# A two-block transformer on one core: gate decays made beside the projection, a gate bias spread in one matmul, row steps placed in VectorE's waits

## The reference, cut to what matters

```python
h = x @ w_in[l]                                  # all columns of the three mixers
# spatial gate: 4 heads of 64, chunks of 128 tokens
v = layer_norm(v, ln_g, ln_b);  w = where(tril, w_s, 0)
z = einsum('hij,bnjhd->bnihd', w, v) + b_s.T[:, :, None];  out_a = u * z
# gated delta rule: 8 heads of 64, chunks of 64
q, k, v = split(silu(causal_short_conv(qkv, conv_w)));  q, k = l2_norm(q) * 64**-0.5, l2_norm(k)
sol = triangular_solve(eye + lower, rhs);  ... then a recurrence over the chunks
# gated attention: 4 heads, keys of 32, values of 64, chunks of 64
log_a = log_sigmoid(g_low @ gate_up + gate_b) / 16
bcum = cumsum(log_a, within a chunk)
q_dec, k_inv, k_dec = q*exp(bcum), k*exp(-bcum), k*exp(bcum[-1]-bcum)
```

## Time and profile before

| | us |
|---|---|
| median of three executions | 3999.43 (3999.33 to 4000.17) |
| profiled execution, its own time | 3998.43 |
| span of the profiled execution, first to last instruction | 3996.6 |
| PE busy | 3807.0 (95%) |
| DVE busy | 2082.7 (52%) |
| ACT busy | 1382.5 (35%) |
| mean granted clock of TensorE, as a share of 2.4 GHz | 0.951 |

### The profile page before, as it was taken

The page is one execution under the profiler, slowest core; times in us unless marked ns, Lnnn a source line. Parts: engine busy times, 40 slices in busy tenths (PEclk is TensorE's granted clock), DMA queues, the critical chain, the costliest instruction groups (busy, mean ns, idle before and its releaser), DMA issues.

```text
span 3996.6 us, 44618 instructions
## 1 busy us (share of the span) xinstructions
PE 3807.0 (95%) x18516; PEld 3137.8 (79%) x18516; DVE 2082.7 (52%) x3673; ACT 1382.5 (35%) x2100; POOL 86.4 (2%) x164
## 2 busy tenths in 40 slices
PE   8998989999999999999999988999999999899998
PEld 5975489999986688888887766888788877577886
DVE  5936757644456543333347467433633374756335
ACT  5434533212356432322226424222322255233222
POOL 0100001111000000000000000000000000000000
PEclk9998999999999999999999958999999999679999
DMA  6410014433320122232222201222222222002222
GB/s 225 151 43 1 1 43 132 125 127 127 103 69 22 43 95 95 99 109 100 96 95 81 78 1 43 95 95 97 85 100 95 96 84 81 15 33 85 95 99 81
DMA packets 92877, 333.35 MB, mean 83 GB/s; under 512 B 11362, under 2 KB 11522, under 8 KB 92420
## 3 DMA queue, kind: packets, MB, share of 16 engines
q1 hardware_dynamic: 77040, 278.10, 20.2%
q0 software_dynamic: 12800, 41.95, 3.4%
q10 hardware_dynamic: 2836, 10.44, 0.7%
HBM read 328.35 MB, written 2.10 MB: 83 GB/s over the span
## 4 chain that ended last, share of the span: by engine, by line
PE 89%; DVE 5%; ACT 5%; issue 1%; DMA 0%; DVEq 0%; ACTq 0%; SPq 0%
PE PS L511 73%; PE PS L1078 2%; PE PS L513 2%; PE PS L1063 1%; PE PS L1094 1%; PE PS L1066 1%; PE PS L1424 1%; PE PS L944 0%; PE PS L2372 0%; PE PS L2168 0%; PE PS L1395 0%; PE PS L716 0%; PE PS L1995 0%; ACT XH L891 0%; DVE H_r L680 0%
## 5 line engine op out<-in xcount | busy, mean ns | idle before, releaser
L511 PE MATMUL PS<-arena_r,ring_hi 128*128 128x512 f32 (+1 forms) x6224 | 2106.0, 377 | 71.2 <-DVE H_r L680 70.1
L511 PE MATMUL PS<-arena_r,ring_r 128*128 128x512 f32 (+1 forms) x4752 | 1781.4, 375 | 0.0
L511 PEld LDWEIGHTS PS<-arena_r,ring_hi 128*128 128x128 f32 x6224 | 1168.4, 189 | 253.3 <-DVE H_r L680 61.9
L511 PE MATMUL PS<-H_r,ring_hi 128*128 128x512 f32 (+1 forms) x3280 | 1231.3, 375 | 0.0
L511 PEld LDWEIGHTS PS<-arena_r,ring_r 128*128 128x128 f32 x4752 | 897.6, 189 | 131.9
L380 DVE TENSOR_TENSOR ring_r<-ring,ring_hi 128x1024 fp32r<-128x1024 f32 x514 | 627.7, 1222 | 660.5 <-ACT ring_hi L371 660.0
L371 ACT ACTIVATE ring_hi<-ring 128x1024 fp32r<-128x1024 f32 x514 | 541.9, 1056 | 875.3 <-DMA ring<-weights_dram 867.5
L511 PEld LDWEIGHTS PS<-H_r,ring_hi 128*128 128x128 f32 x3280 | 622.9, 190 | 95.5 <-issue 3.1
L1654 ACT ACTIVATE arena<-PS 128x512 f32<-128x512 f32 x88 | 52.7, 598 | 532.6 <-PE PS L511 532.6
L1232 DVE SCALAR_TENSOR_TENSOR XH<-PS,mods,XH 128x256 f32<-128x256 f32 (+1 forms) x144 | 68.5, 524 | 237.3 <-PE PS L511 237.3
L1658 DVE SCALAR_TENSOR_TENSOR arena<-arena,PS 128x512 f32<-128x512 f32 x88 | 60.5, 688 | 225.8 <-PE PS L511 225.8
(11 more groups left out here) (370 smaller groups left out, 3164.2 us busy)
## 6 DMA issues: line engine op xcount, KB each, us to landing
ring<-weights_dram SPq DMA_DIRECT2D x526, 512.0 KB, 3.2
rstd<-ada_later_dram POOLq DMA_DIRECT2D x54, 256.0 KB, 2.9
mean<-ada_later_dram POOLq DMA_DIRECT2D x53, 256.0 KB, 3.0
ada_extra<-ada_later_dram POOLq DMA_DIRECT2D x53, 256.0 KB, 3.0
XH<-xT_dram ACTq DMA_DIRECT2D x1, 3072.0 KB, 20.2
ring<-weights_dram ACTq DMA_DIRECT2D x4, 512.0 KB, 4.1
out_dram<-XH SPq DMA_DIRECT2D x8, 256.0 KB, 2.0
con<-second_dram ACTq DMA_DIRECT2D x1, 1536.0 KB
```

The source lines that it names most:

```text
L511: ins = pe.matmul(PS[:, o.bank, 0:hi - lo], w[:, 0, :], x, **flags)
```

## The change

What it does, in the order of the diff:

1. In the projection the gate matmul of the gated attention is issued beside tile 4, the gate logs (four activations) beside tile 5 on ACT, and the minimum, the scaling and the running sum beside tile 6 on DVE. Results go to `silu_ctx` and `ada_extra`. They leave the shared stage.
2. The row turn, the key turn and the value turn, with what ACT and DVE do for them, are written one tile later.
3. The bias of the spatial gate is loaded as two rows, and one matmul for each half of the heads writes it into the bank before the products, which add to it; the products of the two heads of a half alternate.
4. On DVE the weights are masked before the wait for ACT's compaction, and the row steps are divided differently among the other parts: 2, 5, 5, 6 and 13 in place of 10, 14 and 7.

```diff
@@ in_plan
+            t[4]["beside_pe"] = lambda pe: gla_gate_pe(pe, l, gates)
+            t[5]["beside_act"] = lambda act: gla_gate_act(act, l)
+            t[6]["beside_dve"] = lambda dve: gla_gate_dve(dve)
...
-            t[14]["beside_pe"] = lambda pe: turn_rows_pe(pe, l)
-            t[15]["beside_act"] = lambda act: (turned_rows_act(act), high_rows_act(act))
-            t[16]["beside_pe"] = lambda pe: turn_keys_pe(pe, l)
-            t[17]["beside_dve"] = lambda dve: (key_rows_dve(dve, l), low_rows_dve(dve))
-            t[19]["beside_pe"] = lambda pe: turn_values_pe(pe, l)
-            t[20]["beside_dve"] = value_rows_dve
+            t[15]["beside_pe"] = lambda pe: turn_rows_pe(pe, l)
+            t[16]["beside_act"] = lambda act: (turned_rows_act(act), high_rows_act(act))
+            t[17]["beside_pe"] = lambda pe: turn_keys_pe(pe, l)
+            t[18]["beside_dve"] = lambda dve: (key_rows_dve(dve, l), low_rows_dve(dve))
+            t[20]["beside_pe"] = lambda pe: turn_values_pe(pe, l)
+            t[21]["beside_dve"] = value_rows_dve
...
+        gate_arg, gate_log = silu_ctx[:, 0:512], silu_ctx[:, 512:1024]
+        def gla_gate_pe(pe, l, gates):
+            pe.wait_ge(small_loaded.sem, 64 + 48 * l)
+            pe.wait_ge(evac["dve"].sem, gates.freed)
+            pe.matmul(PS[:, 0, :], gup[0:16, :], gl[0:16, :], start=True, stop=True).then_inc(ga_low.sem, 1)
+        def gla_gate_act(act, l):
+            act.wait_ge(ga_low.sem, ga_low.next("act"))
+            a_link(act, nc.scalar.activation(gate_arg, PS[:, 0, :], ACT.Identity, bias=V("gla_gb", l)))
+            a_link(act, nc.scalar.activation(gate_log, gate_arg, ACT.Abs))
+            a_link(act, nc.scalar.activation(gate_log, gate_log, ACT.Exp, scale=-1.0))
+            nc.scalar.activation(gate_log, gate_log, ACT.Ln, bias=V("one")).then_inc(ga_log.sem, 1)
+        def gla_gate_dve(dve):
+            dve.wait_ge(ga_log.sem, ga_log.next("dve"))
+            v_link(dve, nc.vector.scalar_tensor_tensor(out=gate_arg, in0=gate_arg, scalar=0.0, in1=gate_log, op0=ALU.min, op1=ALU.subtract))
+            v_link(dve, nc.vector.tensor_scalar(gate_log, gate_arg, 1.0 / 16.0, None, ALU.mult))
+            nc.vector.tensor_tensor_scan(ada_extra[:], C("rs64", 0, 512), gate_log, 0.0, ALU.mult, ALU.add)
...
+        PAIR = con2_r[:, SELP:SELP + P].bitcast(F32)
...
-        bc, e1, e2, kdec = (area(4096 + 512 * i, 512) for i in range(4))
+        bc = ada_extra[:]
+        _, e1, e2, kdec = (area(4096 + 512 * i, 512) for i in range(4))
@@ units_pe
-            pe.wait_ge(small_loaded.sem, 64 + 48 * l)
-            pe.matmul(PS[:, 4, :], gup[0:16, :], gl[0:16, :], start=True, stop=True).then_inc(ga_low.sem, 1)
...
-            for h in range(4):
-                o = 64 * (h % 2)
+            for q in range(2):
+                pe.matmul(PS[:, q, :].rearrange("p (n t) -> p n t", n=NLT), PAIR[0:2], bs_row[0:2, P * q:P * q + P].unsqueeze(1).to_broadcast([2, NLT, P]),
+                          start=True, stop=False, skip_group_check=True)
                 for n in range(NLT):
-                    dst = PS[o:o + 64, h // 2, P * n:P * n + P]
-                    pe.matmul(dst, vt(n, slice(64 * h, 64 * h + 64)), wsT[:, h, :], start=True, stop=False)
-                    ins = pe.matmul(dst, C("ones")[0:1, 0:64], bs_row[0:1, P * h:P * h + P], start=False, stop=True)
+                    for j in range(2):
+                        h = 2 * q + j
+                        ins = pe.matmul(PS[64 * j:64 * j + 64, q, P * n:P * n + P], vt(n, slice(64 * h, 64 * h + 64)), wsT[:, h, :],
+                                        start=False, stop=True, skip_group_check=True)
@@ units_act
-            act.wait_ge(so_ld.sem, so_ld.next("act"))
-            act.wait_ge(ga_low.sem, ga_low.next("act"))
-            a_link(act, nc.scalar.activation(bc, PS[:, 4, :], ACT.Identity, bias=V("gla_gb", l)))
-            a_link(act, nc.scalar.activation(e1, bc, ACT.Abs))
-            a_link(act, nc.scalar.activation(e1, e1, ACT.Exp, scale=-1.0))
-            nc.scalar.activation(e1, e1, ACT.Ln, bias=V("one")).then_inc(ga_log.sem, 1)
@@ gla_decay_dve
-            dve.wait_ge(ga_log.sem, ga_log.next("dve"))
-            v_link(dve, nc.vector.scalar_tensor_tensor(out=bc, in0=bc, scalar=0.0, in1=e1, op0=ALU.min, op1=ALU.subtract))
-            v_link(dve, nc.vector.tensor_scalar(e2, bc, 1.0 / 16.0, None, ALU.mult))
-            v_link(dve, nc.vector.tensor_tensor_scan(bc, C("rs64", 0, 512), e2, 0.0, ALU.mult, ALU.add))
@@ solve_dve
+            mask_w_dve(dve, l)
             dve.wait_ge(so_d.sem, so_d.next("dve", 4))
-            nc.vector.transpose(LD, D_.rearrange("p q (j t) -> p t q j", j=8)).then_inc(so_ld.sem, 1)
+            ins = nc.vector.transpose(LD, D_.rearrange("p q (j t) -> p t q j", j=8))
+            ins.then_inc(so_ld.sem, 1)
+            dve.wait_ge(so_ld.sem, so_ld.next("dve"))
             centre_v_dve(dve)
+            rows_dve_of_inverse(dve, 0, 2)
             gla_decay_dve(dve)
-            mask_w_dve(dve, l)
+            rows_dve_of_inverse(dve, 2, 7)
             norm_v_dve(dve, l)
             gla_products_dve(dve)
-            rows_dve_of_inverse(dve, 0, 10)
+            rows_dve_of_inverse(dve, 7, 12)
             gla_states_dve(dve)
-            rows_dve_of_inverse(dve, 10, 24)
+            rows_dve_of_inverse(dve, 12, 18)
             sgu_out_dve(dve)
             gla_mask_dve(dve)
-            rows_dve_of_inverse(dve, 24, 31)
+            rows_dve_of_inverse(dve, 18, 31)
@@ third_loads
-                act.dma_start(bs_row[0:1, :], sgub_d[l:l + 1]).then_inc(small_loaded.sem, 16)
+                act.dma_start(bs_row[0:2, 0:2 * P], sgub_d[l].rearrange("(q j t) -> j q t", q=2, j=2)).then_inc(small_loaded.sem, 16)
```

## The result

| | before | after |
|---|---|---|
| median on one chip, us | 3999.38 (3996.74 to 4000.17, 4 executions) | 3972.28 (3964.97 to 3974.40, 4 executions) |
| ratio after to before, 95% interval | | 0.9931 (0.992 to 0.9943) |
| profiled execution, its own time / span, us | 3998.43 / 3996.6 | 3964.97 / 3963.2 |
| DVE busy, ACT busy, us | 2082.7, 1382.5 | 2080.1, 1388.4 |
| mean granted clock of TensorE | 0.951 | 0.957 |

27.1 us less; forecast were 31.4 less, 3968.0. The number came out close, but not by the steps that were forecast. The table cuts both profiles at the same points of the program; a cell gives the length before, then after.

The account below looks back on a forecast made before the run. PE was taken to bound the shared stage in one layer, DVE in the other, with PE waiting for ACT's roots in the projection. 2 x 5.09 + 1.7 + 8.1 + 2.07 + 9.4 = 31.4 us less, 3968.0; range 3960 to 3979.

Parts of the forecast that it names:

- Row turn a tile later: Projection: PE's 4.48 us wait for ACT's roots and 1.65 us of slow clock behind it go, 6.13 us a layer.
- the rival in which ACT comes late to it: Projection: ACT's roots come late to the row turn, 4.0 to 7.3 us lost in both layers, 3972 to 3975; chance 0.10.
- Gate work in the projection: Gate matmul beside tile 4 costs 1.04 us a layer; 6.4 us of gate logs fit 7.3 us of ACT's cover.
- Start of the shared stage: Up to the scaling of v: 1.7 us less in the first layer, 2.07 us in the second.
- Mixing: Spatial gate on PE, shared stage: 9.2 us in place of 17.3; bounds 5 at the higher clock, 12.8 to 14.
- Halves overlap; that rival: Mixing: the rival said halves don't overlap, 12.8 to 14 us in place of 9.2, total 3975 to 3978; chance 0.10.
- Row steps: DVE, shared stage: steps moved into its waits; second layer's scaling of v to output takes 22.9 us, 9.4 less.
- the rival in which the steps only change places: Shared stage: edits do nothing because another engine waits next; only the projection's 10.2 us remain, 3989; chance 0.04.
- Behind the output: End of the shared stage: length kept, as the inverses are there 1.3 us before the 12.57 us of output end.
- the quicker: Output and behind: TensorE's faster clock is granted sooner, 1.3 and 3 us better a layer, 3959 to 3965; chance 0.12.
- slower rival: Behind the output: clock stays at 1.2 GHz, 16.8 us more a layer plus mix projection tiles, up to 4034; chance 0.03.
- The sum: Both layers together: 31.4 us less, 3967.0 by the profiled execution, 3968.0 by the median; given 0.61.

Follow-up runs that it names:

- run 3: Changed kernel with ScalarE making the high half of tile 16's weight slab ahead of the second roots, not behind them: 3964.30 us, ratio 0.992.
- run 4: Changed kernel with both sets of gate logs made together beside tile 5 and none beside tile 8: 3963.65 us, ratio 0.9918.
- run 9: Changed kernel with the gated attention's gate matmul, logs and running sum back at the start of the shared stage: 3975.03 us, ratio 0.9946.
- run 10: The kernel of run 3 with two more of VectorE's row steps (12 and 13) ahead of the states: 3963.21 us, ratio 0.9906.
- run 5: Changed kernel with the mixing loop and bias load of before, each product followed by its own bias matmul: 3987.04 us.
- run 6: Changed kernel with VectorE's row steps divided as before (0 to 10, 10 to 24, 24 to 31): 3992.73 us.
- run 2: Kernel before with only the row, key and value turns moved a tile later: 3995.09 us, ratio 0.9991.

## Why the prediction came out as it did

**Row turn a tile later (-6.1 a layer): the step that failed.** The text had the wait go with 0.97 us to spare, and of what follows it said that the inputs keep their distance and that the weight halves "are made three slabs ahead of PE". For the row turn the reckoning was right: PE begins it at 2212.02 with no idle time ahead, so the rival in which ACT comes late to it did not occur. But the text asked which instructions read the roots, and not what stands behind the roots in ACT's list. By the trace of before the new wait could have been had. There the chain has the roots (start us, us, what):

```profile
2213.12 2.20 ACT arena L1738 x4
```

and the timeline of DVE the low half of tile 16's slab, which ends at 2219.9:

```profile
2218.71 1.23 DVE L380 TENSOR_TENSOR ring_r<-ring,ring_hi 128x1024 fp32r<-128x1024 f32 x1 [9.38 <-ACT ring_hi L371]
```

PE ends tile 14 at 2215.36 - 4.48 = 2210.9, so it would ask for tile 16 at 2210.9 + 5.45 + 0.66 = 2217.0; the slab follows the roots (end 2215.3) by a load, an evacuation, a silu, a high and a low half, 1.28 + 0.60 + 0.52 + 0.95 + 1.24 = 4.6, thus 2219.9. That is a wait of 2.9 us; 3.2 were measured, with the slow clock behind it. Runs 3 and 4 give 4.9 and 4.8 us a layer back, each by another edit.

**Gate work in the projection.** Right. The matmul takes 1.05 us (forecast 1.04), and ACT's second roots end 1.2 us later, of which 1.05 are PE's. ACT's idle time covered the logs. Each load again takes 1.28 us with the next activation 0.01 us behind it, so the drain of 1.38 us that the Trainium skill (ScalarE: Activation LUTs, "What ACT_TABLE_LOAD costs") adds to a load shows in no row here either.

**Start of the shared stage.** Right: 1.5 and 2.1 us against 1.7 and 2.07, and run 9 loses 2.2. Steps 0 to 7 fit ahead of the scaling of v, with 3.0 us of DVE's wait left there. The "over 7 us" that DVE was said to wait was a misreading: it idled 1.31 and 3.46 us in the first layer, and 7 is reached only with the 2.4 us of the three instructions that leave.

**Mixing: the term that was mis-sized.** 9.2 us were taken, at 1.2 GHz throughout; it took 4.2, at a granted clock of 1.00, which is under even the 5 that the text gave as its bound for the quick clock. At 1.2 GHz (run 10) it takes 7.9: the bias matmuls 2.07 each as forecast, four alternating pairs 1.98, thus 0.49 a pair in place of the 0.63 to 0.70 read from L1991. So PE isn't the later engine in the first layer, and the stretch is DVE's 22.8 in place of 25.1, 2.2 us better than the sum. Halves overlap; that rival is out: in the kernel before, where products did not alternate, a single one already took 0.62 us from its start to the next start at that clock:

```profile
2350.99 0.69 PE L1977 MATMUL PS<-con,XH 128*64 128x128 f32 x2
2351.61 0.69 PE L1978 MATMUL PS<-scratch,con 1*64 1x128 f32 x2
```

**Row steps.** Right: 22.84 against 22.9 in the second layer, 32.27 with the steps back. That both engines had to be relieved is shown by runs 5 and 6; the rival in which the steps only change places is out.

**Behind the output.** Right: the inverses were there in time (12.53 us as before), and the clock stayed where it was, 0.50 in the output and 0.64 against 0.66 behind it; neither the quicker nor the slower rival occurred.

**The sum.** 31.4 - 10.3 (projections) + 2.0 (shared stage) + 2.6 (forming, at a clock of 0.78 in the window shown, 0.50 at the same place before) - 0.8 (behind the output) + 3.1 (the rest of the program, unchanged) = 28.0 us from the first projection on. That the time came near the forecast is luck: the stretches of the sum, with the one behind the output, gave 22.4 us (23.3 - 0.1 - 0.8) in place of 31.4, since the shared stage won back only 2.0 of the 10.3 us lost in the projections, and the 5.7 us that bring it near lie in code that the change doesn't touch. They are not shown to be the change's: among the runs on the changed kernel, forming the matrices took 26.7 to 28.6 us and the program between the two layers 825.3 to 828.3, in the two profiles without the change 28.3 to 28.7 and 828.4. Whether the change makes the shorter lengths likelier stays open.

## What to carry to other kernels

When a wait for one engine's result is removed by asking later, look at everything that stands behind that result in the engine's list, and find which of it is needed next: here the list stayed as long as it was, and only its reader changed. Where two engines bound a stretch at nearly the same length, relieve both in one edit: tested alone, each looks worth little (runs 5 and 6). An instruction that feeds the next tile goes ahead of a long batch for which there is time.

## What the runs showed of the hardware

The same code ran at either level of TensorE's clock in different executions: the seven key products took 1.96 or 3.57 to 3.75 us, the mixing 4.2 to 7.9, and the unchanged program ahead of the first projection of the second block between 2126 and 2145 us. The Trainium skill (TensorE: Matmul & The Clock Gate, "What's actually happening") says that the point at which the level changes depends on a phase that the program does not set, so that the same kernel differs from run to run. That it differs these runs show; what sets it none of them shows. Behind a pause of 3.2 us PE's next 5.6 us ran at a granted clock of 0.70 in one run and 0.50 in another (runs of the changed kernel and 2), and without the pause at 1.00 (run 3).
